# Gate columns of both first layers as pairs of seven products, by way of DRAM, and a new order of small steps and turns in attention

## The reference

```python
p = h @ w_in                       # h: modulated rms norm of x; hc of ctx the same
o_mla  = block_attention(q_mla, [k_mla, k_mla_c], [v_mla, v_mla_c])   # 6 heads, keys 96 wide
o_gqa  = block_attention(q_gqa, [k_gqa, k_gqa_c], [v_gqa, v_gqa_c])   # 6 heads, keys 64 wide
o_conv = conformer_conv(p[..., OFF_CONV:OFF_GATE], ...)   # a * sigmoid(g), depthwise taps (31), norm, silu, 256x256
y = concat([o_mla, o_gqa, o_conv]) * silu(p[..., OFF_GATE:])          # 1024 gate columns
x_new = x + gate * (y @ w_out)
```

```python
y = lax.conv_general_dilated(y, dw_w[:, None, :], window_strides=(1,), padding=((15, 15),),
                             dimension_numbers=('NWC', 'WIO', 'NWC'), feature_group_count=256) + dw_b
```

## Time and profile before

| what | us |
|---|---|
| median of 3 runs | 4684.64 |
| lowest and highest run | 4683.93, 4687.36 |
| the profiled execution, device time | 4684.99 |
| its span, first to last instruction | 4683.1 |
| PE busy | 4501.9 |
| DVE busy | 2380.1 |
| ACT busy | 1272.8 |

### The profile page before, as it was taken

One profiled execution on the slowest core, in us unless ns is written; L12 is line 12 of the kernel. 1 busy time (PEld: TensorE's weight loads), 2 busy tenths in 40 slices (PEclk: granted clock), 3 DMA queues, 4 the chain that ended last, 5 costly groups with the idle time before them and its releaser, 6 DMA issues.

```text
span 4683.1 us, 46821 instructions
## 1 busy us (share of the span) xinstructions
PE 4501.9 (96%) x19044; PEld 2422.8 (52%) x19044; DVE 2380.1 (51%) x3952; ACT 1272.8 (27%) x2006; POOL 46.7 (1%) x66
## 2 busy tenths in 40 slices
PE   8998999999998999999999999999999999999997
PEld 3554566655444676544456745555544444444443
DVE  6466556633275556424982222333543555556554
ACT  2003445423004445323012312333300311110033
POOL 1000000000000000000000000000000000000000
PEclk9999999999999999999999999999999999999998
DMA  7200000021110000100111000000011211111112
GB/s 266 92 27 18 1 1 1 1 92 60 39 33 10 1 1 1 71 23 23 41 36 32 28 27 23 19 14 19 19 45 59 72 41 45 45 45 57 51 50 67
DMA packets 46319, 187.17 MB, mean 40 GB/s; under 512 B 4704, under 2 KB 4704, under 8 KB 44320
## 3 DMA queue, kind: packets, MB, share of 16 engines
q1 hardware_dynamic: 35040, 131.09, 8.7%
q0 software_dynamic: 11072, 53.15, 3.1%
HBM read 174.78 MB, written 9.44 MB: 39 GB/s over the span
## 4 chain that ended last, share of the span: by engine, by line
PE 91%; DVE 4%; ACT 3%; issue 1%; DMA 0%; POOL 0%; ACTq 0%; DVEq 0%; PEld 0%; PEldq 0%; SPq 0%; POOLq 0%
PE psum L2373 20%; PE psum L403 9%; PE psum L1214 7%; PE psum L1392 5%; PE psum L2053 5%; PE psum L1644 5%; PE psum L1242 5%; PE psum L689 5%; PE psum L1228 4%; PE psum L2327 3%; PE psum L1757 2%; PE psum L1747 2%; PE psum L2339 2%; PE psum L2069 2%; PE psum L1784 2%; PE psum L2096 1%
## 5 line engine op out<-in xcount | busy, mean ns | idle before, releaser
L2373 PE MATMUL psum<-arena 128*128 128x512 f32 x2184 | 937.9, 592 | 0.9 <-DVEq L386 0.9
L2373 PEld LDWEIGHTS psum<-arena 128*128 128x128 f32 x2184 | 414.8, 190 | 523.2 <-issue 521.9
L1214 PE MATMUL psum<-arena 64*128 64x512 f32 (+3 forms) x1200 | 393.6, 539 | 15.2 <-ACT arena L1169 14.1
L403 PE MATMUL psum<-arena 128*128 128x512 f32 (+1 forms) x1040 | 403.0, 550 | 1.4 <-DMA arena<-stream 1.4
L2678 DVE TENSOR_TENSOR arena<-arena,psum 128x512 f32<-128x512 f32 x280 | 192.5, 688 | 397.1 <-PE psum L2373 388.5
L1311 DVE TENSOR_REDUCE arena<-psum 128x1 f32<-128x1280 f32 (+1 forms) x216 | 290.7, 1367 | 114.9 <-PE psum L1214 114.9
L1228 PE MATMUL psum<-arena 128*128 128x128 f32 x1968 | 301.4, 280 | 26.0 <-ACT arena L1285 11.7
L1228 PEld LDWEIGHTS psum<-arena 128*128 128x128 f32 x1968 | 228.3, 142 | 178.9 <-issue 119.6
L403 PEld LDWEIGHTS psum<-arena 128*128 128x128 f32 x1040 | 197.4, 190 | 205.6 <-issue 198.0
L1280 ACT ACTIVATE arena<-psum,arena 128x1280 f32<-128x1280 f32 (+1 forms) x216 | 265.1, 1232 | 127.7 <-DVE arena L1311 127.6
L1285 ACT ACTIVATE arena<-psum 128x512 f32<-128x512 f32 x294 | 170.7, 596 | 321.2 <-PE psum L1228 320.8
(11 more groups left out here) (292 smaller groups left out, 5051.8 us busy)
## 6 DMA issues: line engine op xcount, KB each, us to landing
arena<-stream SPq DMA_DIRECT2D x228, 512.0 KB, 3.7
arena<-mod_t POOLq DMA_DIRECT2D x32, 512.0 KB, 4.6
arena<-mod_w POOLq DMA_DIRECT2D x4, 2048.0 KB, 26.3
arena<-stream SPq DMA_DIRECT2D x6, 1024.0 KB, 9.8
arena<-x SPq DMA_DIRECT2D x4, 1280.0 KB, 16.4
arena<-x POOLq DMA_DIRECT2D x2, 2048.0 KB, 19.2
x_mid<-arena POOLq DMA_DIRECT2D x2, 2048.0 KB, 8.7
arena<-x_mid POOLq DMA_DIRECT2D x2, 2048.0 KB, 19.5
```

What stands on the lines that cost most here:

```text
L403: last = nc.tensor.matmul(ps(slot * SLOT + c0, n), lhsT=sb(w + k * P, P), rhs=rhs(k, c0, n), start=k == 0, stop=k == nk - 1)
L1214: last = nc.tensor.matmul(ps(s * SLOT + c0, n), lhsT=q, rhs=keys, start=True, stop=True)
L2373: last = nc.tensor.matmul(ps(pair_bank(j, p), HALF), lhsT=lhsT(k), rhs=rhs(k), start=k == 0, stop=k == nk - 1)
```

## The change

The eight gate blocks become four more pairs, blocks 13 to 20 of `proj{l}`. Since the sums of data and weights lie at Y_AT, their outputs can't go there: each pair is assembled in a staging area (STAGED_AT, over part of the tables and T2_AT), ACT applies Silu to both halves in one instruction, and POOL stores them to a DRAM tensor `gated`. ACT moves nothing of the next gate pair before the store has landed. Once all four have, SP reloads the table columns that the staging overwrote, waits for them, and loads all gates from DRAM to Y_AT; `rope(0)` waits for the tables and `mixed(0)` for the gates. The convolution's pairs now come first (blocks 5 to 8), and the 30 further taps are no loop: they stand in DVE's program five to a pair, in the six pairs behind the convolution's. The other part is the order in attention: the small grouped steps of the first layer stand behind all wide grouped ones, and the step behind a preparation also turns two groups first.

```diff
-        counts += [(f"proj{l}", 13), (f"gate{l}", 8), (f"out{l}", 8)]
+        counts += [(f"proj{l}", 21), (f"out{l}", 8)]
...
-    PROJECT_TILES = [GK_AT, GV_AT, GQ_AT + 2 * TC, CKV_AT, KR_AT, CQ_AT, CQ_AT + TC, GQ_AT, GQ_AT + TC, ACC_AT, ACC_AT + TC, ACC_AT, ACC_AT + TC]
+    STAGED_AT = TAB_AT + T + 512
+    PROJECT_TILES = [GK_AT, GV_AT, GQ_AT + 2 * TC, CKV_AT, KR_AT] + [ACC_AT, ACC_AT + TC] * 2 + [CQ_AT, CQ_AT + TC, GQ_AT, GQ_AT + TC] + \
+        [STAGED_AT, STAGED_AT + TC] * (KD // 2)
+    CONVOLUTIONS, FIRST_GATE = (5, 7), 13
...
         for a in project_pairs(l):
             pair(a)
-        g = BLOCKS[f"gate{l}"]
-        cols = chunks(layer_shapes(l))
-        for m in range(KD):
-            if m < 2:
-                t.eng.wait_ge(product_read.sem, PROJECT_READ[l, a, 7 if m == 0 else 3])
...
-            pe_block(t, g + m, (m + 1) % 2, h, cols, waits=m >= 2)
...
-            convolution = PROJECT_TILES[a] == ACC_AT
-            if a == PROJECT_BLOCKS - 2:
+            m = (a - FIRST_GATE) // 2
+            if a == CONVOLUTIONS[1]:
                 t.eng.wait_ge(glu_used.sem, t.next(glu_used))
+            if a == FIRST_GATE:
+                nc.scalar.preload_act_table(ACT.Silu)
+            elif a > FIRST_GATE:
+                t.eng.wait_ge(stored.sem, 16 * (4 * l + m))
...
-        for m in range(KD):
-            t.eng.wait_ge(block_done[(g + m) % 2].sem, uses(g + m))
-            nc.scalar.activation(sb(Y_AT + m * TC, width), ps((m + 1) % 2 * SLOT, width), ACT.Silu).then_inc(psum_free[(m + 1) % 2].sem, 1)
+            if m >= 0:
+                both = sb(STAGED_AT, 2 * TC).rearrange("p (s c) -> p s c", c=TC)[:, :, 0:width]
+                nc.scalar.activation(both, both, ACT.Silu).then_inc(gate_ready.sem, 1)
...
             s1, u2, u3 = c21, c12, c22
+            taps(a, 2)
             p2 = product(a, 2)
             t.eng.wait_ge(first_copied.sem, PROJECT_FIRST[l, a, 1])
             combine(c11, s1, p2, ALU.add, product_read)
             combine(u2, s1, product(a, 6), ALU.add, product_read)
+            taps(a, 1)
             combine(u3, u2, product(a, 7), ALU.add, product_read)
             weight_sum(a + 2, 3)
+            taps(a, 1)
             combine(c21, u3, product(a, 4), ALU.add, product_read)
             p5 = product(a, 5)
             combine(c22, u3, p5, ALU.add)
             combine(u2, u2, p5, ALU.add, product_read)
             weight_sum(a + 2, 1)
             weight_sum(a + 2, 2)
+            taps(a, 1)
             combine(c12, u2, product(a, 3), ALU.add, product_read)
             weight_sum(a + 2, 4)
...
+            if i == 0:
+                t.eng.wait_ge(sp_in[3].sem, tables_back(l))
...
+            if m == 0:
+                t.eng.wait_ge(sp_in[3].sem, gates_back(l))
...
-                if l == 0:
+                if l == 0 and kind == "mla":
                     steps += [(kind, p, QT + j, QT, C // P, None) for j in range(C // P)]
+        if l == 0:
+            steps += [("gqa", p, QT + j, QT, C // P, None) for p in range(3) for j in range(C // P)]
...
-        return 2 if u + 1 < len(steps) and steps[u + 1][0] == "gqa" else 0
+        grouped_next = u + 1 < len(steps) and steps[u + 1][0] == "gqa"
+        return 2 if grouped_next or (u and steps[u - 1][5]) else 0
...
+        def gates_in(l):
+
+            t.eng.wait_ge(stored.sem, 16 * 4 * (l + 1))
+            eng.dma_start(sb(TAB_AT + T, 2 * T), io["tables"][:, T:3 * T]).then_inc(sp_in[3].sem, 16)
+            t.eng.wait_ge(sp_in[3].sem, tables_back(l))
+            gates, y = (a.rearrange("p (k c) -> p k c", c=TC)[:, :, 0:layer_shapes(l)] for a in (io["gated"], sb(Y_AT, KD * TC)))
+            eng.dma_start(y, gates).then_inc(sp_in[3].sem, 16)
...
+            for m in range(KD // 2):
+                t.eng.wait_ge(gate_ready.sem, t.next(gate_ready))
+                gates, staged = (a.rearrange("p (k c) -> p k c", c=TC)[:, :, 0:layer_shapes(l)]
+                                 for a in (io["gated"][:, 2 * m * TC:2 * (m + 1) * TC], sb(STAGED_AT, 2 * TC)))
+                eng.dma_start(gates, staged).then_inc(stored.sem, 16)
```

67 lines of the change are left out of this document (36 added, 31 removed).

## The result

The changed kernel takes 4648.34 us (median of 4 runs, 4647.58 to 4649.42) against 4685.55 us before (4 runs, 4683.93 to 4687.36): a ratio of 0.9922 with a 95% interval of 0.9907 to 0.9936, so **37.2 us or 0.8% faster**. The prediction said 4658.6 us, 26 us faster, in a range of 4648 to 4670: the direction is right, the time lies at the range's lower edge, and 11 us of gain have to be explained.

A forecast was written before the change was run, and what follows sets the result against it. PE, busy 91% of the span, was taken as the bound. Terms of -27.4, -1.4, +5.5, +4.0, -4.9 and -1.8 gave -26.0 us against 4684.99, so 4659.0, or 4658.6 us against the median; range 4648 to 4670.

The forecast's parts named there:

- Pairs, weight wait and end of project: Project stages: gate blocks as pairs -27.4 us, no wait for first gate weights -1.4, later start of heads +5.5.
- Stores and return from DRAM: Gate pairs and start of heads: storing the gates, then reloading tables and gates, holds nothing up; cost 0.
- The ring: Gate pairs' cycle of Silu, store, move and DVE work: 26.8 us inside 30.94 (first layer), 22.1 inside 24.07 (second).
- Rival 1: Project: stores pace the gate pairs, slower than before from stores of 13.0 us on; 4742 us at 22.5; chance 0.05.
- Rival 2: Heads: gates return late from DRAM, DVE waits 8 us in the first layer, some 3 in the second; 4670; chance 0.08.
- Small steps last: First layer's grouped attention: moving small steps to the end saves 6.4 us, lower clock gives back 1.5; -4.9 us.
- The clock at the start of heads: Heads' opening: PE restarts at a lower clock after the longer gap, 2 us lost a layer; +4 us.
- The +6 us: Start of heads, both layers: upper bound of the clock term if every such restart runs at the low clock.
- Turns ahead: Attention, behind four preparations: turns fill PE's wait, at most 0.87 us each, half comes back; -1.8 us.

The follow-up runs named there:

- the changed kernel of the second group: The changed kernel measured again, unedited, on the chip of the kernels with a filled gap ahead of heads and a shorter tail: 4651.27 us, ratio 0.9928.

## Why the prediction was right, and where it was off

**Pairs, weight wait and end of project: right.** The two stretches were forecast at -11.8 and -11.5 us and measured -12.0 and -11.3. The gaps ahead of heads were to be 4.7 and 3.4 and are 4.82 and 3.60.

**Stores and return from DRAM: right at 0.** The ring was sized well, as the doubled stores show: margins of 2 and about 5 us where 2 and 4 stood. Rival 1 has its mechanism, but not its condition: it needs stores that count from 13 us on, and they took 4.7 and 5.4. Three chained stores of 5.0 us each put s at 15: its formula gives 3 x 4.7 + 3 x 8.0 = 38 us, and 44 were measured against the changed kernel of the second group, enough to be slower than before. The page of that rival, the Trainium skill's "SBUF — State Buffer", section "Who interferes with whom", warns of DMAs from GpSimd's queue that starve beside a DVE copy; next to the taps no store did, by the landings just given. Rival 2 is out: 5 MB came back in 15.1 us, faster than either rate that was drawn on; SP had no other load in flight beside it.

**Small steps last: the total right, in part by luck.** 2.86 us each where 2.9 stood, and 1.3 us given back in the first wide step (11.78 us instead of 10.51, the window at 753 above with a clock of 0.50) where 1.5 stood. The place of that loss was wrong: it was expected in the small steps, which run at full speed. And it is not the edit's: the second execution of the changed kernel has 10.51 us there, and its grouped stage is 6.4 us shorter than before, not 5.1. The prediction also read the 11.78 us interval of the earlier trace rows as the softmax of the next wide step alone. The granted clock is 0.50 in it (842.6 to 846.0, the window at 843 above) and in its counterpart (917.7 to 921.1), while the wide step behind the last small latent ones, at full speed, takes 10.51. So about 2.7 of the 18 us that two such places cost were half speed.

**The clock at the start of heads: the mechanism held, the step to its price failed.** Both stages open at 0.50, and DVE's first read comes 2.2 and 1.7 us later, close to the 2 that the prediction took. The step that failed is that this delay runs on to the end of the stage: it is 0.5 and 0.7 us there. Of the rest, 0.7 and 1.1 us came back at once because the later centring no longer met POOL (3.75 to 3.02 us and 3.56 to 2.48); the second layer is settled by that. In the first, 0.3 us more came back before `rope(0)`, where an idle stretch of DVE of 0.51 us is gone, and DVE is 1.2 us late from there on. The last 0.7 us were no gain of the edit: the kernel before lost them. There PE ran at half speed from 453.4 to 460.3, and DVE waited for it, as its timeline shows:

```profile
467.39 1.23 DVE L1045 TENSOR_TENSOR arena<-arena 128x1024 f32<-128x1024 f32 x1 [1.15 <-PE psum L906]
```

In the changed kernel that half speed lasts from 442.2 to 445.6 and DVE waits for nothing. The kernel with turns ahead alone shows the same without any edit ahead of it: 3.4 us of half speed, no wait, and heads of 67.36 us instead of 68.07. In all fourteen traces this wait is there where the stretch lasts 6.8 us and absent where it lasts 3.4. The Trainium skill, "TensorE: Matmul & The Clock Gate", section "HAM oscillation — how this bites in real kernels", is right here that both restarts run slow (granted clock 0.50). The +6 us drawn from it is further off than the 4 of the sum, and with the clock kept full in this place the kernel was no faster; half speed came 10 to 13 us later there instead.

**Turns ahead: the step that failed most.** "If the shorter gap spares a drop of the clock, it is about 1.5 us more for each; I count none." Three of four were spared: -5.7 us instead of -1.8, the largest part of the 9.5 us by which the spans' difference beats the sum. Against the one interval that had no half speed before (22.83 to 22.41) the turns gain 0.4 us; the other three gain 2.1, 1.6 and 1.6. Useless filling gave the same 1.6 twice, so in the second layer all of it is the clock. That a shorter gap is what spares half speed is likely but not shown: it stayed away once behind the full 2.14 us, and it came back once with the turns ahead. The earlier trace rows show the one preparation that had full speed: behind 2.57 us of idleness two matmuls take 1.12 us. Behind the next, 94 us later in the same trace, the same matmuls take 1.33 and the four turns after them 1.06 instead of 0.60. One preparation had been taken for all four.

**Not counted: the opening and the first step of attention.** They gave 0.9 and 1.5 us. The half-speed stretch in the first step was 6.8 us long before and 3.4 after, which is the size of the 1.5; what made it shorter was not tried, and in the three kernels with filling in heads or with POOL's wait the step took 30.7 us again, with 6.8 us of half speed. With turns ahead alone there was none, and the step took 27.93. The 0.9 us stand before anything that was edited and are left as scatter between executions. The same program ran again at a median 2.9 us higher. Between its two traces half speed moved by 1.7 us in one place, 1.3 and 1.7 us the other way in two, and 3.3 us in the last stage, so a few of the 37 us depend on where half speed happens to fall.

In sum: -26.0 forecast; -2.8 for the clock at heads, -3.9 for turns ahead, -0.2 for the grouped steps, and -2.6 for what was not counted make the -35.5 measured on the spans.

## What to carry to other kernels

Before a stage is costed, look at the granted clock behind every instance of a small idle gap, not behind one of them: an idle gap of about 2 us may or may not be followed by half speed, and a few matmuls in it, useful or not, were worth 1.6 us each here. When a gain fails to arrive at the end of a stage, look at what now runs beside what; a delayed engine can dodge a conflict, and a repaired one can run into it. Move a GpSimd operation that reads SBUF away from the critical VectorE instructions with two SBUF inputs: one wait gave 3.3 us in one stage, half of it in those instructions and half because PE then waited less and kept its clock. And before the whole difference of two medians is credited to an edit, see in which stages it lies: as much again came from a stage that the edit did not touch.

## What the runs showed of the hardware

- **DVE stands still behind POOL.** Two DVE instructions with two SBUF inputs (128x1280, f32) take 3.02 us alone, 3.75 to 4.23 when the end of POOL's three multiplications overlaps their start, and 7.13 when most of them do: each time about what was left of POOL's run, and then 3.02. All of the delay lies in the first of the two, 5.61 us instead of 1.49 in the last case, and it outlasts an end and a new start within POOL's three. POOL's own time is 6.87 us in all these cases, and 7.66 where it starts during the centring. A DVE instruction that reads only PSUM keeps its 1.49 us beside POOL. The Trainium skill, "SBUF — State Buffer", section "Who interferes with whom", says that a DVE instruction with two SBUF inputs and a GpSimd instruction that reads SBUF contend, and the traces agree.
- **Half speed is not tied to a gap alone.** The gap of 2.14 us in the second layer was followed by 3.4 us of half speed before the change, by 6.8 with the small steps moved and once by none with the gate pairs alone; the 2.57 us of the first layer once by none; and the same program had a drop at 632 us in one execution and none in another. An edit in one stage so moves the time of others by 1.6 us a place, which is why the parts alone were read by their intervals and not by medians.
- **Writes to DRAM were cheap.** Stores of 1 and 1.25 MB from POOL's queue landed in 5.4 and 4.7 us beside a busy DVE, and a 5 MB load with the queue to itself in 15.1 us, some 347 GB/s.
